# The last stage of a two-layer kernel with its matmul operands exchanged: token blocks as the loaded weights, 512 columns of expert rows as the moving operand

## The reference

```python
q = rmsnorm(h, gain) @ w_q                       # 8 heads, two halves of 128
s = scores of the halves against 2 x 128 sub-keys; top 16 of each; top 16 of the sums
gate = softmax(top 16 scores)                    # expert e = 128 * i + j
out = h + sum over picks of gate * gelu(x . peer_u[e]) * peer_v[e]
```

## Time and profile before

| | |
|---|---|
| median of 3 runs | 2228.89 us (2228.45 to 2229.49) |
| profiled execution: its time | 2229.13 us |
| profiled execution: its span, first to last instruction | 2227.5 us |
| granted TensorE clock, mean | 0.997 of full |
| busy: PE, PEld, DVE, ACT, POOL | 98%, 87%, 71%, 48%, 23% of the span |

### The profile page before, as it was taken

How to read it: one execution, slowest core, us unless ns; L and a number is a source line. 1 busy time by engine, 2 the same in 40 slices (tenths; PEclk the granted TensorE clock), 3 DMA queues, 4 the chain that set the end, 5 groups by cost and what they waited for, 6 DMA issues and landing times.

```text
span 2227.5 us, 35099 instructions
## 1 busy us (share of the span) xinstructions
PE 2172.6 (98%) x12499; PEld 1931.4 (87%) x12499; DVE 1592.3 (71%) x3258; ACT 1067.6 (48%) x1942; POOL 505.6 (23%) x389
## 2 busy tenths in 40 slices
PE   6999999999999988899999999999999999999999
PEld 4888888888878545687899999999999999999999
DVE  5444444433367687464489899999988899999996
ACT  5344434322243477644455535888854333333332
POOL 0000000000030000010100222655435555555550
PEclk9999999999999999999999999999999999999999
DMA  4232222222234200023466889999999999999993
GB/s 175 92 94 94 85 85 85 93 96 94 94 102 173 73 1 1 1 67 95 128 182 172 272 267 309 369 402 386 390 342 406 412 401 389 393 398 386 394 406 137
DMA packets 134241, 475.74 MB, mean 214 GB/s; under 512 B 14448, under 2 KB 30832, under 8 KB 132192
## 3 DMA queue, kind: packets, MB, share of 16 engines
q1 hardware_dynamic: 74592, 232.29, 30.8%
q0 software_dynamic: 55920, 212.36, 24.9%
q10 hardware_dynamic: 3600, 29.36, 3.2%
HBM read 422.58 MB, written 50.86 MB: 213 GB/s over the span
## 4 chain that ended last, share of the span: by engine, by line
PE 90%; DVE 6%; ACT 2%; issue 1%; DMA 0%; ACTq 0%; DVEq 0%
PE bank L474 18%; PE bank L475 17%; PE bank L476 17%; PE bank L1203 8%; PE bank L1204 8%; PE bank L1205 8%; PE bank L1175 4%; PE bank L489 2%; PE bank L589 1%; PE bank L549 1%; DVE wlo L461 1%; DVE rows L2244 1%; PE bank L783 1%; PE bank L801 1%; ACT pair_prob L1429 1%; PE bank L766 1%
## 5 line engine op out<-in xcount | busy, mean ns | idle before, releaser
L474 PE MATMUL bank<-act_hi,whi 128*128 128x352 f32 (+1 forms) x1840 | 660.3, 359 | 9.2 <-DVE act_lo L1703 5.4
L461 DVE TENSOR_TENSOR wlo<-raw,whi 128x1024 fp32r<-128x1024 f32 x398 | 484.8, 1224 | 251.0 <-ACT whi L457 241.0
L475 PE MATMUL bank<-act_lo,whi 128*128 128x352 f32 (+1 forms) x1840 | 650.2, 353 | 0.0
L476 PE MATMUL bank<-act_hi,wlo 128*128 128x352 f32 (+1 forms) x1840 | 649.7, 353 | 0.0
L457 ACT ACTIVATE whi<-raw 128x1024 fp32r<-128x1024 f32 x398 | 418.7, 1057 | 389.3 <-PE bank L1205 330.9
L474 PEld LDWEIGHTS bank<-act_hi,whi 128*128 128x128 f32 x1840 | 346.0, 188 | 51.6 <-issue 15.7
L476 PEld LDWEIGHTS bank<-act_hi,wlo 128*128 128x128 f32 x1840 | 345.8, 188 | 32.7
L475 PEld LDWEIGHTS bank<-act_lo,whi 128*128 128x128 f32 x1840 | 346.2, 188 | 31.2 <-issue 0.5
L1203 PE MATMUL bank<-h_hi,whi 128*128 128x384 f32 x1024 | 342.2, 334 | 1.8 <-issue 1.8
L1205 PE MATMUL bank<-h_hi,wlo 128*128 128x384 f32 x1024 | 342.1, 334 | 0.0
L1204 PE MATMUL bank<-h_lo,whi 128*128 128x384 f32 x1024 | 342.1, 334 | 0.0
(11 more groups left out here) (397 smaller groups left out, 2779.5 us busy)
## 6 DMA issues: line engine op xcount, KB each, us to landing
raw<-tiles SPq DMA_DIRECT2D x398, 512.0 KB
gates_dram<-stage ACTq DMA_DIRECT2D x12, 2048.0 KB
wg<-gates_dram POOLq DMA_DIRECT2D x16, 1536.0 KB
acts_dram<-gelu SPq DMA_DIRECT2D x120, 192.0 KB
hf<-acts_dram POOLq DMA_DIRECT2D x30, 768.0 KB, 7.7
bias<-alibi POOLq DMA_DIRECT2D x16, 256.0 KB, 2.9
w1s<-cmp_w POOLq DMA_DIRECT2D x1, 4096.0 KB, 13.3
res<-x_t ACTq DMA_DIRECT2D x4, 512.0 KB, 6.1
```

The lines of the kernel that those rows point to most:

```text
L461: dve.tensor_tensor(wlo[:, j.slot, :], raw[:, j.slot, :], whi[:, j.slot, :].bitcast(F32), ALU.subtract).then_inc(lo_made, 1)
L474: pe.matmul(to, wh, x, start=(kc == 0), stop=False)
L475: pe.matmul(to, wh, xl, start=False, stop=False)
L476: last = pe.matmul(to, wl, x, start=False, stop=(kc == KC - 1))
```

## The change

In stage V the operands are exchanged. The gated values of 128 tokens (`h_hi` or `h_lo`, 128 experts x 128 tokens) are loaded as weights, and 512 of the 1024 columns of the expert tile pass. The 384 tokens are three blocks, so there are six sums (block x half), in banks 6, 7, 4, 5, 2, 3, with tokens as partitions. A tile takes 18 matmuls of 512 columns: for each block, high x `whi`, high x `wlo`, low x `whi`, both halves of each. In the last job each half's three matmuls stand together.

The residual must lie with tokens as partitions too, so 24 more transposes turn it: eight behind each of the U jobs 122, 125 and 126, into banks 6 and 7, 4 and 5, 6 and 7. ScalarE copies each bank back into `res` (six copies of 128 x 512), behind the GELUs of jobs 124, 125 and 126. The first tile of stage V waits for the last copies out of the banks that its blocks use. At the end VectorE makes six additions of 512 columns into `done_rows`, which lies in free ring slots of `whi`, and SyncE's queue stores them, 256 KB each, as rows of 2 KB. Two semaphores of an earlier stage are merged into others.

```diff
+        def sum_bank(tb, half):
+            return bank[(6, 7, 4, 5, 2, 3)[2 * tb + half]]
+        def rest(tb, half):
+            return res[:, 4 * half:4 * half + 4, tb * P:(tb + 1) * P]
+        def done_slot(tb):
+            return (JOBS + 1 + tb) % RING
...
+            for tb in range(DT // P):
+                for half in range(2):
+                    sp.wait_ge(S("summed"), 2 * tb + half + 1)
+                    sp.dma_start(out_rest[tb * P:(tb + 1) * P, half * T:(half + 1) * T],
+                                 done_rows[:, done_slot(tb), half, :]).then_inc(stored, 16)
+            sp.wait_ge(stored, 16 * (1 + 2 * DT // P))
...
-                last.then_inc(S("vb_turned"), 1)
+                last.then_inc(v_turned, 1)
...
+            def turn_rest(tb, b):
+                for dc in range(KC):
+                    last = turn(pe, bank[b + dc // 4][:, (dc % 4) * P:(dc % 4 + 1) * P],
+                                res[:, dc, P + tb * P:2 * P + tb * P], ident)
+                last.then_inc(S("rest_turned"), 1)
...
+                if n == U_REST + 2:
+                    turn_rest(0, 6)
+                if n == U_REST + 5:
+                    pe.wait_ge(own_step, 3)
+                    turn_rest(1, 4)
+                if n == U_REST + 6:
+                    pe.wait_ge(S("rest_copied"), 2)
+                    turn_rest(2, 6)
...
-                x, xl = h_hi[buf][:, m, :], h_lo[:, buf, m, :]
...
-                for dc in chunks:
-                    w = slice(dc * P, (dc + 1) * P)
-                    wh, wl, to = whi[:, j.slot, w], wlo[:, j.slot, w], bank[dc][:, 0:DT]
...
-                    pe.matmul(to, wh, x, start=(n == 0), stop=False)
-                    pe.matmul(to, wh, xl, start=False, stop=False)
-                    last = pe.matmul(to, wl, x, start=False, stop=(n == P - 1))
+                for tb in range(DT // P):
+                    if n == 0:
+                        pe.wait_ge(S("rest_copied"), (6, 4, 6)[tb])
+                    if n == 0 and tb == 2:
+                        for late in (4, 3):
+                            was_taken(pe, Job(J_V - late))
+                    tokens = slice(tb * P, (tb + 1) * P)
+                    x, xl = h_hi[buf][:, m, tokens], h_lo[:, buf, m, tokens]
+                    steps = [(by, w, half) for by, w in ((x, whi), (x, wlo), (xl, whi)) for half in range(2)]
                     if n == P - 1:
-                        last.then_inc(own_step, 1)
+                        steps.sort(key=lambda step: step[2])
+                    for at_, (by, w, half) in enumerate(steps):
+                        ends = n == P - 1 and at_ % 3 == 2
+                        last = pe.matmul(sum_bank(tb, half)[:, :], by, w[:, j.slot, half * T:(half + 1) * T],
+                                         start=(n == 0 and at_ < 2), stop=ends)
+                        if ends:
+                            last.then_inc(own_step, 1)
...
+                for tb, at_, b in ((0, 4, 6), (1, 5, 4), (2, 6, 6)):
+                    if n == U_REST + at_:
+                        act.wait_ge(S("rest_turned"), tb + 1)
+                        for half_ in range(2):
+                            copy(rest(tb, half_), bank[b + half_][:, :].rearrange("p (k d) -> p k d", k=4),
+                                 S("rest_copied"))
...
-            for dc in range(KC):
-                dve.wait_ge(own_step, 8 + dc)
-                dve.tensor_tensor(res[:, dc, P:T], res[:, dc, P:T], bank[dc][:, 0:DT], ALU.add)\
-                    .then_inc(S("summed"), 1)
+            for tb in range(DT // P):
+                for half_ in range(2):
+                    dve.wait_ge(own_step, 8 + 2 * tb + half_)
+                    dve.tensor_tensor(done_rows[:, done_slot(tb), half_, :].rearrange("p (k d) -> p k d", k=4),
+                                      rest(tb, half_), sum_bank(tb, half_)[:, :].rearrange("p (k d) -> p k d", k=4),
+                                      ALU.add).then_inc(S("summed"), 1)
```

More of the change, by code:

```diff
@@ L1372, in _ @@
             for b in range(2):
-                act.wait_ge(S("vb_turned"), b + 1)
-                copy(vtb[:, b, :, :], bank[4 + b][:, :].rearrange("p (t v) -> p t v", t=TT), S("vtb_copied"))
+                act.wait_ge(v_turned, KC + b + 1)
+                copy(vtb[:, b, :, :], bank[4 + b][:, :].rearrange("p (t v) -> p t v", t=TT), vtok_copied)
             for m in (12, 13):
@@ L2555 @@
     r = run_bass_kernel_spmd(nc, [arrays], core_ids=[0])
[L2556 to L2557 removed]
+    return np.ascontiguousarray(np.concatenate([r.results[0]["out_rows"], r.results[0]["out_rest"]], 0)[None])
```

19 lines of the change are left out of this document (4 added, 15 removed).

## The result

| | before | after |
|---|---|---|
| median of its runs | 2229.10 us (2228.45, 2228.89, 2229.31, 2229.49) | 2213.03 us (2211.48, 2212.26, 2213.81, 2221.66) |
| ratio of the times, 95% interval (the medians alone: 0.9928) | | 0.9936 (0.9921 to 0.9951) |
| profiled execution: time, span | 2229.13, 2227.5 us | 2221.66, 2220.0 us |

The changed kernel is 16 us faster in the median, where 7 were forecast, and 2213.0 lies outside the range (2220.0 to 2227.0). But the execution that was profiled took 2221.66 us, half a microsecond from the 2222.1 forecast for it.

A forecast was written before the change was run, and what follows sets the result against it. The prediction took TensorE's stream, busy 98% of the span, as the bound; -10.0 (stream) + 2.6 (turning) + 0 + 0.4 (end) = -7.0 us gave a median of 2221.9 us (2222.1 profiled), range 2220.0 to 2227.0.

The forecast's parts named there:

- the stream: Last stage on TensorE: a tile's 18 matmuls of 512 columns cost 4.082 us instead of 4.160; -10.0 us.
- The rival from 352 columns: Last stage: a line through 352 and 384 columns prices a 512-column matmul at 0.2329 us, ending at 2235.9; chance 0.06.
- The rival of price by columns alone: Last stage: a matmul has no fixed part, so the stage is unchanged, ending at 2231.9; chance 0.12 with half-way cases.
- the estimate from the section of the Trainium skill: Warm matmul gap of N/2.4 + 2.5 ns: the last stage gains only 2.0 us, ending at 2229.9.
- the turning: Three groups of eight residual transposes in TensorE's stream before the last stage, 0.87 us each; +2.6 us.
- the copies and the waits: ScalarE's six copies, 3.6 us, fit where it waits for TensorE; waits for freed banks are over in time; cost 0.
- the seam: TensorE's idle gap before the last stage stays 1.77 us, cost 0; rival: up to 2 us more, chance 0.10.
- The end: Last additions and stores: a later start, a longer addition and 64 KB more to move; +0.4 us, bounds 0 to +1.0.
- The sum: All terms together, -10.0 + 2.6 + 0 + 0.4 = -7.0 us.
- the transfers: Rival in the last stage: DMA, needing 402 GB/s, becomes the pace, ending at 2226 to 2229; chance 0.05.
- VectorE took over: Rival in the last stage: VectorE, at 3.80 of 4.08 us a tile, becomes the pace; chance 0.02.

The follow-up runs named there:

- e8: The changed kernel with each 512-column matmul of the last stage cut into two of 256 columns with the same loaded block; 2248.37 us.
- e4: The changed kernel without the 24 transposes and their six copies, the residual added unturned (output wrong); 2210.40 us.
- e1_again: The changed kernel run again unchanged, 12 executions; 2217.49 us, six at 2211 to 2214 and six at 2221 to 2224.
- e5: The changed kernel with one 128 x 128 transpose behind each of the 48 groups of gate matmuls; one level, 2217.92 us.
- e9: The kernel before with the same 48 transposes as e5; one level, 2225.92 us.
- e7: The changed kernel without the 384 matmuls that make the gates (output wrong); one level, 2208.20 us.
- e11: The kernel before, run once more unchanged for a trace; 2230.31 us.
- e10: The changed kernel with each group of gate matmuls moved inside the next job, ahead of its seventh block; 2220.35 us, spread from 2213.81 to 2223.58.
- e2: The changed kernel with the three matmuls of a bank together in every job; 2221.32 us, five executions at 2211 to 2214, seven at 2221 to 2224.
- e12: The changed kernel with a 128 x 128 transpose behind every eighth group of gate matmuls, six in all; 2216.92 us.
- e13: The changed kernel with a single 128 x 128 transpose behind the 24th of the 48 groups of gate matmuls; one level, 2217.43 us.
- e14: The changed kernel with two transposes in a row behind the 24th group of gate matmuls; 2217.14 us, three executions at 2212.4, nine at 2216.6 to 2218.9.
- e16: The changed kernel with two transposes in a row behind the first group of gate matmuls; 2213.46 us, five executions at 2211.8 to 2214.4, one at 2223.06.
- e17: The kernel before with two transposes in a row behind the first group of gate matmuls; 2221.45 us, ten executions at 2218.4 to 2222.3, two at 2230.5.
- e15: The changed kernel with one more ordinary 352-column matmul behind the 24th group of gate matmuls; two levels, median 2218.58 us.
- e6: The changed kernel with one 24 x 24 transpose behind each of the 48 groups of gate matmuls; one level, 2230.14 us.
- e3: The changed kernel with the loaded block changed at five of six matmuls and the bank at four of six; 2214.14 us.

## Why the prediction was right, and where it was wrong

**Right: the stream (-10.0; measured -10.28).** The step of 0.2268 us, read in an earlier stage at 94 GB/s, was 226.7 ns under 401 to 405 GB/s, in three orders of the matmuls. The rival from 352 columns, 0.2329 at 512, would have given 430 matmuls per 100 us; there were 443. The rival of price by columns alone falls by e8: 12.8 ns of a matmul are fixed, and halving the columns of each matmul cost 30.8 us. By the estimate from the section of the Trainium skill cited in the prediction (page "TensorE: Matmul & The Clock Gate", section "Back-to-back issue gap"; 2.5 ns fixed) the end would have been 2229.9; the traces disagree with it at all three sizes (it gives 109.2, 162.5 and 215.8 ns, measured 120.0, 173.3 and 226.7).

**Right: the turning (+2.6; +2.64),** with the copies and the waits hidden (e4), and **the seam (0; 0.00)**. **The end (+0.4; +0.29)** lay within its bounds. Neither the transfers nor VectorE took over: no idle time of TensorE, 92 to 93 of 100 for VectorE as forecast. The sum, -7.0, compares with -7.5 and -7.6 in the two pairs of traces at equal level, with -7.8 and -8.8 from e1_again's medians, and with -8.0 from e5 against e9. The three terms together are -7.3 us in every pair of traces, within 0.1. What the totals differ from that, up to 1.5 us either way, arises ahead of the parts that the change touches: stage U begins anywhere from 1082.2 to 1085.0 us in the nineteen traces, and what scatters there was not followed.

**Wrong: the step from the sum to a time.** The sum was right and the time was not: "So 2222.1 by the profiled execution and 2221.9 as a median" takes the spread of the runs shown, 1 us, for that of the kernel, and "about 0.2% (4.5 us) is what a measurement of this kernel can tell from no change" does so again. The kernel before has two levels 9 us, 0.4%, apart, and lay on the upper in 91 of the 133 executions beside the experiments; the runs shown were all from it. A measurement of a few executions can therefore miss by 9 us either way, and this one did: -16 where equal levels give -7.5 to -8.8. That the profiled execution took 2221.66, so near to the 2222.1, was luck of the draw too: three of four took the other level. The range had a bound for each cost of the change and none for a stretch that it doesn't touch. What was missing is a second case 9 us below the first.

The trace held the warning. Just ahead of the row a step takes 0.167 us, and behind it 0.1585, for the same instruction on the same operands. The prediction took the 0.1585 as the price of 352 columns, for the rival, without asking what the jobs with gates in the same stage paid. Their steps, 0.1668 us in the timeline of before above, would have shown that one form had two prices with the clock and the transfers the same.

**Not settled.** Shown: the two rhythms in the 48 jobs with gates make the 9 us; they hold over hundreds of matmuls; one 128 x 128 transpose turned one into the other each time in two traces, and an ordinary matmul did not; the long one also stands where there are no groups of gates (e7, e11). The traces place the choice behind TensorE's waits between 1310 and 1385 us and not at the execution's start, as all nineteen are short up to 1310. Not shown: what decides at such a wait, what several transposes in a row do, why e10 switched without either, and why 3 of 18 stayed long. The experiment that is missing takes those few waits away or adds one more, and looks whether the share of the levels moves. That the rhythm lies in how weight loads and matmuls interlock is a guess; the loads' records show 188 ns at either.

## What to carry to other kernels

Price a matmul by the distance of its starts in a window of the same size, and where two sizes are known, split it into a fixed part and a part per column: here 12.8 ns and 0.418 ns, so that fewer, wider matmuls over the same columns gain the fixed part only, and whatever brings the data into the new layout must be cheaper than that (2.6 of 10 us here).

Before a gain of half a per cent is believed, look at the executions one by one: if they fall into groups, compare group with group, or give both kernels something that puts them on one level. And when one form of instruction shows two prices within a trace, find what stands where it changes before using either.

## What the runs showed of the hardware

- A stream of 352-column float32r matmuls runs at 158.2 or at 166.6 ns a step, at granted clock 1.00 in both. Among the groups of gates one of the two holds through all 48 jobs, at DMA share 1.01 in either (changed kernel and e2). Where TensorE had waited between two jobs, the rhythm changed in 46 of 117 places; where it neither waited nor made transposes, twice in some 1800 (e2, e10).
- One 128 x 128 transpose turned the rhythm over each time in the two traces where that can be seen (e12, e13); a pair left it short in the three traces with one (e14, e16, e17), but not in all executions; an ordinary matmul left it as it was (e15). The job directly behind one 128 x 128 transpose was short in either case, at 158.2 or 158.7 ns (e5, e9, e12).
- A 128 x 128 transpose costs 0.12 us in this stream; one of 24 x 24 costs 0.26 us more (e5, e6; 0.38 in all).
- How often the bank and the loaded block change makes no difference to a 512-column stream: 443 per 100 us with six, two and four changes of the bank and two, four and five of the block in six matmuls (changed kernel, e2, e3). A 256-column stream runs at 120.0 ns a step, though each matmul has a weight load whose record shows 192 ns (e8): the records of the loads overlap one another as well as the matmuls.
